# A new order of work for ScalarE, VectorE and TensorE in the SSD mixers of a four-layer encoder kernel

## The chip, the cores and the metric

The kernel runs on one core of one Trainium2 chip. The metric is the device time of one execution in microseconds (us); less is better. The instruction streams of the engines are written out by hand, one per engine, and meet only at semaphores, so each engine works strictly through its own list.

## The reference

A trunk of four layers over 256 tokens of 1024 features, all in float32. Layer 0 and layer 3 use the bidirectional Mamba-2 SSD mixer, layer 1 a gated short convolution, layer 2 neighbourhood attention; each mixer and each squared-ReLU MLP (1024 to 4096 to 1024) is followed by a LayerNorm of the residual sum. Only the SSD mixer is touched:

```
zxbcdt = x @ w_in                       # 1024 -> 2048 (z) + 4096 (x, B, C) + 64 (dt)
xbc = silu(depthwise_conv(xbc, conv_w) + conv_b)       # 5 taps
dt  = softplus(dt_raw + dt_bias)                       # two directions, 32 heads
y   = ssd(xs, dt, a, B, C) forward + the same backward + d_skip * xs
y   = y * silu(z)                                      # the gate
out = grouped_rmsnorm(y, norm_w) @ w_out               # 8 groups of 256 channels
```

The SSD runs in two chunks of 128 tokens: inside a chunk through a decayed product of C and B, across chunks through a state.

## The kernel before

**Weight units.** All weights, 226 blocks of mostly 128 x 2048 floats (1 MB), pass through one pipeline in the order of `plan_units`. SyncE loads unit u into a ring of three `raw` buffers as soon as unit u - 3 has been split. ScalarE copies it to `w_high` (L997), VectorE writes the remainder `w_low` = raw - w_high (L1338); both rings have four slots, so the split of unit u waits until TensorE has finished unit u - 4 (`w_used`). Three matmuls (high x high, low x high, high x low) stand for one product of full precision. `split_to(u)` on either engine means: split all units up to u, here, in this place of the engine's list. A split is one instruction of some 2 us on each engine, and everything behind it in the list waits for it and for what it waits for.

**Accumulators.** A projection (`project`) of 48 matmuls fills one of two accumulator banks, `acc`; it is freed when its reader has taken it. `result(u)` gives that reader the bank: it first runs `split_to(u + 3)` and only then waits for unit u to be finished on TensorE.

**The SSD mixer** has eight groups. A group has the units z, bc (B and C), x and so (its two row blocks of the output weight). Unit order: dt, z0, bc0, x0, z1, bc1, x1, then z(i), bc(i), x(i), so(i-2) for i = 2 to 6, then bc7, x7, z7, so5, so6, so7. With group i's projections, TensorE's loop of step i (L845 to L857) does the inner work of group i-1:

- project z(i); `state_products` (L800, "cb"); `turn_xs` (L789, "xs", the transpose of the convolved x); project bc(i); `cross_chunk` (L811, "off"); `scan` (L824, "yg"); project x(i); `out_unit` of so(i-2) (L681, "y" banks); `turn_gated` of group i-1 (L835, "op").
- These five inner steps cb, xs, off, yg, op take turns in two banks `inner`. The bank of xs is the one that op of the group before has used, and it is freed when VectorE has read it in `gated_low` (`op_low`, L1488).
- In the last step (i = 7) there is no z projection in the loop; z7 comes after it, and op6, cb7, so5 (in two halves by token tile, t0 and t1), xs7, off7, yg7 follow, then so6 with op7 inside it, then so7 (`tail`).

**ScalarE in step i** (L1188 to L1208): z_tanh(i); copies of cb and xs of group i-1; `shift_decays(i)` (L1091); `start_conv` bc(i) (bank to `conv_pad`, L1062, and the first tap, L1068); tanh of bc; `squares(i-1)`, half of `decays(i)` (L1101), `normalise(i-1)` (L1138); `start_conv` x(i); the other half of decays; tanh of x; `split_to(x(i)+4)`; `gated_high(i-1)` (L1148). z_tanh and start_conv call `result`, so each has a split in front of it.

**VectorE in step i** (L1608 to L1621): silu_z(i) (with a split in front); `decayed_products(i-1)` (L1508 to L1522); `join_decays(i)` (L1498); `add_cross(i-1)` (L1532, L1537); a split, then the taps of bc(i) (L1468, eight instructions); `gate_scan(i-1)` (L1548, L1550); silu of bc(i) (L1480); a split, then the taps of x(i); silu of x(i); `split_to(x(i)+4)`; `gated_low(i-1)` (L1488). The splits before the taps are at L1460.

GpSimd scales xs for the state and for the token itself (L432), raises the mean squares to the power -1/2 and issues the loads of the decays E, whose source is a small table in DRAM that ScalarE stores early in the mixer (L1183).

```
def result(u):                       # ScalarE and VectorE alike
    split_to(u + 3)
    act.wait_ge(w_used, u + 1)
    return acc_of[u]
```

## Time and profile before

| | before |
|---|---|
| median of 3 runs | 1647.73 us (1646.65 to 1647.95) |
| the profiled execution: its own time | 1646.52 us |
| its span, first to last instruction | 1644.6 us |
| mean granted TensorE clock | 0.946 of 2.4 GHz |
| TensorE matmul busy | 1491.3 us (91%) |
| VectorE busy | 991.2 us (60%) |
| ScalarE busy | 767.6 us (47%) |
| first SSD mixer, up to its last output matmul | 0 to 327.5 us of the span |
| second SSD mixer, likewise | about 1141 to 1443.7 us |

Rows of a timeline give start (us), duration (us), engine, line, what is written from what, the number of merged instructions and, in brackets, the idle time of the engine before it and what ended it. "L1338" is line 1338 of the kernel. In rows of stretches the numbers after the length are the busy time and count of instructions of TensorE, its weight loads, VectorE, ScalarE and GpSimd, then the granted clock as a share of 2.4 GHz, the share of the DMA engines and GB/s. Below, xs1 means the transposes of `turn_xs` for group 1, and so on.

### The profile page before, as it was taken

What the parts mean: (1) busy time and instruction counts of PE and PEld (TensorE: products, weight loads), DVE (VectorE), ACT (ScalarE), POOL (GpSimd) and SP (SyncE); (2) the same over time, 40 slices, a digit from 0 to 9 for tenths busy, and PEclk for the clock granted to TensorE, in tenths of its full rate; (3) what the DMA queues carried; (4) which work ended last, traced back from release to release, by engine and by line L of the source; (5) the groups of instructions that cost most, each with busy time, mean ns of one, the idle gap of its engine ahead of it and who ended that gap; (6) DMA issues with size and microseconds to landing.
All of it is one profiled execution on the core that took longest, in us unless ns stands there. A gap on an engine that the chain in (4) does not pass through costs nothing.

```text
span 1644.6 us, 24792 instructions
## 1 busy us (share of the span) xinstructions
PE 1491.3 (91%) x9837; PEld 1379.9 (84%) x9837; DVE 991.2 (60%) x1227; ACT 767.6 (47%) x1103; POOL 163.9 (10%) x245
## 2 busy tenths in 40 slices
PE   6888887799999999999999999999878787799996
PEld 6877887599998999999899799998878787689995
DVE  4767766655456666555754465556776776665554
ACT  3666655344433434443355444433656664435441
POOL 1111110052231000000000000000111120000000
PEclk9899898899999999999999999999999988899998
DMA  7635543346674564555553345555644462336551
GB/s 220 183 126 154 172 138 127 102 147 200 207 218 156 188 210 143 187 195 205 170 171 121 102 138 183 194 203 151 190 152 132 152 179 103 122 110 205 205 179 52
DMA packets 198193, 266.98 MB, mean 162 GB/s; under 512 B 11768, under 2 KB 167824, under 8 KB 198080
## 3 DMA queue, kind: packets, MB, share of 16 engines
q1 hardware_dynamic: 188032, 237.53, 43.6%
q0 software_dynamic: 9200, 27.55, 6.3%
q8 instruction: 79, 1.29, 0.3%
q10 hardware_dynamic: 848, 0.32, 0.1%
q14 instruction: 34, 0.28, 0.1%
HBM read 264.19 MB, written 1.18 MB: 161 GB/s over the span
## 4 chain that ended last, share of the span: by engine, by line
PE 66%; DVE 18%; issue 8%; ACT 7%; DMA 1%; SPq 0%; DVEq 0%; POOL 0%; ACTq 0%
PE acc L557 31%; PE y L681 24%; DVE conv L1468 6%; DVE w_low L1338 6%; PE acc L570 4%; ACT w_high L997 3%; PE y L570 1%; PE inner L789 1%; DMA raw<-in_ssd_w_in 1%; PE inner L811 1%; DVE opT L1488 1%; DVE gate L1550 1%; DVE gate L1548 1%; DVE E L1532 1%; ACT square L1130 1%
## 5 line engine op out<-in xcount | busy, mean ns | idle before, releaser
L557 PE MATMUL acc<-xT,w_high 128*128 128x256 f32 (+1 forms) x3392 | 646.2, 292 | 2.7 <-DVE xT L1399 1.1
L1338 DVE TENSOR_TENSOR w_low<-raw,w_high 128x2048 fp32r<-128x2048 f32 (+1 forms) x226 | 513.1, 2275 | 175.3 <-ACT w_high L997 93.3
L557 PEld LDWEIGHTS acc<-xT,w_high 128*128 128x128 f32 x3392 | 557.3, 201 | 7.8 <-issue 3.5
L997 ACT ACTIVATE w_high<-raw 128x2048 fp32r<-128x2048 f32 (+1 forms) x226 | 428.1, 1898 | 204.5 <-PE y L681 75.4
L557 PE MATMUL acc<-xT,w_low 128*128 128x256 f32 (+1 forms) x1696 | 492.8, 291 | 0.0
L681 PE MATMUL y<-w_high,opT 128*128 128x512 f32 x1408 | 404.3, 397 | 7.9 <-DVE opT L1488 6.0
L557 PEld LDWEIGHTS acc<-xT,w_low 128*128 128x128 f32 x1696 | 339.9, 200 | 0.0
L681 PEld LDWEIGHTS y<-w_high,opT 128*128 128x128 f32 x1408 | 263.9, 191 | 61.4 <-issue 9.5
L681 PE MATMUL y<-w_low,opT 128*128 128x512 f32 x704 | 226.3, 396 | 0.0
L570 PE MATMUL acc<-w_high,xT 128*128 128x256 f32 (+1 forms) x960 | 188.5, 298 | 15.6 <-DVE xT L1399 9.3
L1354 DVE TENSOR_TENSOR opT<-conv,opT 128x512 fp32r<-128x512 f32 x56 | 39.0, 696 | 267.2 <-issue 236.6
L570 PEld LDWEIGHTS acc<-w_high,xT 128*128 128x128 f32 x960 | 160.3, 205 | 19.4 <-issue 16.0
L681 PEld LDWEIGHTS y<-w_low,opT 128*128 128x128 f32 x704 | 134.5, 191 | 29.0
L570 PE MATMUL acc<-w_low,xT 128*128 128x256 f32 (+1 forms) x480 | 141.5, 295 | 0.0
L1468 DVE SCALAR_TENSOR_TENSOR conv<-conv_pad,ssd_par,conv 128x256 f32<-128x256 f32 x256 | 104.1, 479 | 3.4 <-ACT conv L1068 3.4
L1037 ACT ACTIVATE conv<-acc 128x512 f32<-128x512 f32 x60 | 35.8, 597 | 149.3 <-PE acc L557 135.1
L409 POOL TENSOR_TENSOR small<-small,minus_half 128x1 f32<-128x1 f32 x16 | 15.9, 993 | 842.6 <-DVE small L1375 842.6
L570 PEld LDWEIGHTS acc<-w_low,xT 128*128 128x128 f32 x480 | 98.7, 206 | 0.0
L789 PE MATMUL inner<-ident,xsT 128*128 128x128 f32 x64 | 16.1, 400 | 81.0 <-DVE opT L1488 78.5
L789 PEld LDWEIGHTS inner<-ident,xsT 128*128 128x128 f32 x64 | 10.6, 202 | 87.1 <-issue 68.0
L1076 ACT ACTIVATE tanh<-conv 128x512 f32<-128x512 f32 x32 | 20.2, 631 | 135.4 <-DVE conv L1468 135.4
L1024 ACT ACTIVATE xT<-inner 128x512 fp32r<-128x512 f32 x32 | 18.1, 595 | 117.5 <-PE inner L647 117.1
(182 smaller groups left out, 1175.6 us busy)
## 6 DMA issues: line engine op xcount, KB each, us to landing
raw<-in_ffn_w_in SPq DMA_DIRECT2D x128, 512.0 KB, 4.6
raw<-in_ffn_w_out SPq DMA_DIRECT2D x128, 512.0 KB, 4.4
raw<-in_ssd_w_in SPq DMA_DIRECT2D x96, 512.0 KB, 5.1
E<-cumsum_dram POOLq DMA_DIRECT2D x32, 512.0 KB, 5.5
raw<-in_ssd_w_out SPq DMA_DIRECT2D x32, 512.0 KB, 5.8
raw<-in_sc_w_in SPq DMA_DIRECT2D x24, 512.0 KB, 4.6
raw<-in_na_w_qkv SPq DMA_DIRECT2D x24, 512.0 KB, 4.6
raw<-in_sc_w_out SPq DMA_DIRECT2D x8, 512.0 KB, 4.4
```

The source lines that it names most:

```text
L557: mm = nc.tensor.matmul(bank[:, c * SEQ:(c + 1) * SEQ][:, span], w[:, col:col + P], xT[:, k, low, span], start=(k == 0 and part == 0), sto ...
L570: mm = nc.tensor.matmul(bank[:, t * width:(t + 1) * width], xT[:, k, low, t * P:(t + 1) * P], w[:, k * width:(k + 1) * width], start=(k == ...
L681: mm = nc.tensor.matmul(Y[t][c][:, :], opT[:, o % ACTS, low, k, t * P:(t + 1) * P], w[:, k * D + c * 512:k * D + (c + 1) * 512], start=(fi ...
L789: mm = nc.tensor.transpose(bank[:, t * GW + c * P:t * GW + (c + 1) * P], xsT[:, m % 2, c, t * P:(t + 1) * P], ident[:, :])
L811: mm = nc.tensor.matmul(bank[:, t * GW:(t + 1) * GW], cross[m % 2][:, (1 - t) * P:(2 - t) * P], xs_end[:, (1 - t) * GW:(2 - t) * GW], star ...
L997: nc.scalar.activation(w_high[:, u % SPLIT, 0:k * c], raw[:, u % RAW, 0:k * c], ACT.Copy).then_inc(w_high_done, 1)
L1024: nc.scalar.activation(xT[:, 4 * half:4 * half + 4, 0, t * P:(t + 1) * P], bank[:, :].rearrange("p (k c) -> p k c", k=4), ACT.Copy).then_i ...
L1037: nc.scalar.activation(conv[:, o % 2, :, :], views(bank[:, :]), ACT.Relu).then_inc(relu_done, 1)
L1076: nc.scalar.activation(th[:, m % 2, :], src, ACT.Tanh, scale=scale).then_inc(tanh_done, 1)
L1338: V.tensor_tensor(w_low[:, u % SPLIT, 0:k * c], raw[:, u % RAW, 0:k * c], f(w_high[:, u % SPLIT, 0:k * c]), ALU.subtract).then_inc(w_low_d ...
L1354: V.tensor_tensor(low, src, high, ALU.subtract).then_inc(op_low, 1)
L1468: ins = V.scalar_tensor_tensor(out=y, in0=pad[:, c % 2, i, q:q + SEQ], scalar=tap(j, q, ct), in1=y, op0=ALU.mult, op1=ALU.add)
```

## The change

`result` is parted in `split_to` and a new `finished(u)`, which only waits for unit u. In the SSD mixers the readers of the accumulators (`start_conv`, `z_tanh`, `silu_z`) use `finished`, and `taps` has no split any more; the splits become calls of their own behind the reader, each of unit u + 4 behind the reading of unit u. `gated_high` and `gated_low` stand ahead of the splits of step i. At both ends of the mixer the order changes: group 0 is transposed (op0) in step 2, behind z2; the last step is written out, with bc7 ahead of cb6 and x7 between xs6 and off6, and op6 behind the first half of so5. The other mixers and the MLP keep `result`.

```diff
 # TensorE
-                    for i in range(1, G):
-                        if i < G - 1:
-                            project(names[("z", i)], range(NT))
+                    for i in range(1, G - 1):
+                        project(names[("z", i)], range(NT))
+                        if i == 2:
+                            turn_gated(0)
                         state_products(i - 1)
                         turn_xs(i - 1)
                         project(names[("bc", i)], range(NT))
                         cross_chunk(i - 1)
                         scan(i - 1)
                         project(names[("x", i)], range(NT))
-                        if i < G - 1:
-                            if i >= 2:
-                                out_unit(s, names[("so", i - 2)], first=(i == 2))
+                        if i >= 2:
+                            out_unit(s, names[("so", i - 2)], first=(i == 2))
                             turn_gated(i - 1)
+                    project(names[("bc", G - 1)], range(NT))
+                    state_products(G - 2)
+                    turn_xs(G - 2)
+                    project(names[("x", G - 1)], range(NT))
+                    cross_chunk(G - 2)
+                    scan(G - 2)
                     project(names[("z", G - 1)], range(NT))
-                    turn_gated(G - 2)
                     state_products(G - 1)
+                    turn_xs(G - 1)
                     o = n["opu"]
                     n["opu"] += 1
                     out_part(s, names[("so", G - 3)], o, False, False, [0])
-                    turn_xs(G - 1)
-                    out_part(s, names[("so", G - 3)], o, False, False, [1]).then_inc(w_used, 1)
+                    turn_gated(G - 2)
                     cross_chunk(G - 1)
                     scan(G - 1)
+                    out_part(s, names[("so", G - 3)], o, False, False, [1]).then_inc(w_used, 1)
                     out_unit(s, names[("so", G - 2)], between=lambda: turn_gated(G - 1))
 # ScalarE (start_conv and z_tanh: finished in place of result)
+                    split_to(names[("dt", 0)] + 4)
                     z_tanh(0)
-                    split_to(names[("bc", 0)] + 3)
...
                     start_conv("bc", 0)
...
+                    split_to(names[("z", 0)] + 4)
                     conv_tanh()
+                    split_to(names[("bc", 0)] + 4)
                     start_conv("x", 0)
+                    split_to(names[("x", 0)] + 4)
                     conv_tanh()
                     shift_decays(0)
                     for i in range(1, G):
                         if i < G - 1:
                             z_tanh(i)
-                        if i == 1:
-                            decays(0, early)
-                            decays(0, late)
+                            if i == 1:
+                                decays(0, early)
+                                decays(0, late)
+                            if i == 2:
+                                gated_high(0)
+                        else:
+                            start_conv("bc", i)
+                            split_to(names[("bc", i)] + 4)
                         copy_cross(i - 1)
                         copy_xs(i - 1)
+                        if i < G - 1:
+                            split_to(names[("z", i)] + 4)
                         shift_decays(i)
-                        start_conv("bc", i)
-                        conv_tanh()
+                        if i < G - 1:
+                            start_conv("bc", i)
+                            split_to(names[("bc", i)] + 4)
+                            conv_tanh()
+                        else:
+                            conv_tanh()
+                            start_conv("x", i)
                         squares(i - 1)
                         decays(i, early)
                         normalise(i - 1)
-                        start_conv("x", i)
+                        if i < G - 1:
+                            start_conv("x", i)
                         decays(i, late)
+                        split_to(names[("x", i)] + 4)
                         conv_tanh()
-                        split_to(names[("x", i)] + 4)
                         if i == G - 1:
-                            z_tanh(G - 1)
-                        gated_high(i - 1)
-                    copy_cross(G - 1)
-                    copy_xs(G - 1)
-                    split_to(names[("so", G - 1)] + 1)
+                            z_tanh(i)
+                            copy_cross(i)
+                            copy_xs(i)
+                            split_to(names[("z", i)] + 4)
+                        if i >= 2:
+                            gated_high(i - 1)
+                            split_to(names[("so", i - 2)] + 4)
                     squares(G - 1)
                     normalise(G - 1)
-                    split_to(names[("so", G - 1)] + 2)
                     gated_high(G - 1)
 # VectorE (silu_z: finished in place of result; taps: no split)
...
+                    split_to(names[("dt", 0)] + 4)
                     silu_z(0)
-                    split_to(names[("bc", 0)] + 3)
                     dve.wait_ge(cs_acc, mixer + 1)
...
+                    split_to(names[("z", 0)] + 4)
                     silu_bc(0, taps("bc", 0))
-                    silu_x(0, taps("x", 0))
+                    split_to(names[("bc", 0)] + 4)
+                    y = taps("x", 0)
+                    split_to(names[("x", 0)] + 4)
+                    silu_x(0, y)
...
                     for i in range(1, G):
                         if i < G - 1:
                             silu_z(i)
...
+                            if i == 2:
+                                gated_low(0)
+                            decayed_products(i - 1)
+                            split_to(names[("z", i)] + 4)
+                            join_decays(i)
+                            add_cross(i - 1)
+                            y = taps("bc", i)
+                            gate_scan(i - 1)
+                            silu_bc(i, y)
+                            split_to(names[("bc", i)] + 4)
+                        else:
+                            y = taps("bc", i)
+                            decayed_products(i - 1)
+                            split_to(names[("bc", i)] + 4)
+                            silu_bc(i, y)
+                            join_decays(i)
+                            add_cross(i - 1)
+                            gate_scan(i - 1)
                         silu_x(i, taps("x", i))
-                        split_to(names[("x", i)] + 4)
                         if i == G - 1:
-                            silu_z(G - 1)
-                        gated_low(i - 1)
-                    decayed_products(G - 1)
-                    split_to(names[("so", G - 1)] + 1)
+                            silu_z(i)
+                            split_to(names[("x", i)] + 4)
+                            decayed_products(i)
+                            split_to(names[("z", i)] + 4)
+                        if i >= 2:
+                            gated_low(i - 1)
+                            if i < G - 1:
+                                split_to(names[("x", i)] + 4)
+                            split_to(names[("so", i - 2)] + 4)
+                        else:
+                            split_to(names[("x", i)] + 4)
                     add_cross(G - 1)
                     gate_scan(G - 1)
-                    split_to(names[("so", G - 1)] + 2)
                     gated_low(G - 1)
```

## Rows read from the trace of the kernel before

**Rows 1.** Stretches of the second mixer (xs1 to xs2, ...) and of an MLP
```profile
core 0: us, PE busy (x) PEld busy (x) DVE busy (x) ACT busy (x) POOL busy (x), PEclk, DMA share, GB/s
...
1214.89:1247.91 33.02, 28.81 (x200) 27.26 (x201) 21.91 (x37) 20.28 (x39) 4.17 (x6) 0.92 0.40 128
...
1349.58:1383.63 34.05, 24.12 (x153) 22.57 (x153) 23.93 (x38) 17.97 (x37) 5.26 (x6) 0.80 0.45 155
1383.63:1418.28 34.65, 27.20 (x188) 26.16 (x189) 21.82 (x37) 18.43 (x38) 2.93 (x4) 0.84 0.28 93
1418.28:1443.67 25.39, 22.01 (x88) 17.40 (x88) 14.09 (x23) 6.74 (x11) 3.73 (x5) 0.83 0.37 123
400.00:500.00 100.00, 100.00 (x623) 90.58 (x622) 54.17 (x39) 44.37 (x36) 29.70 (x47) 1.00 0.70 208
```

**Rows 2.** TensorE's timeline in a group of the first mixer: the inner steps
```profile
208.09 1.03 PE L811 MATMUL inner<-ring_a,E 128*128 128x256 f32 x4
...
221.97 0.60 PE L835 MATMUL inner<-ident,gate 128*128 128x128 f32 x4
...
228.15 1.03 PE L800 MATMUL inner<-ring_a 128*128 128x256 f32 x4
233.37 1.09 PE L789 MATMUL inner<-ident,xsT 128*128 128x128 f32 x4 [4.19 <-DVE opT L1488]
```

**Rows 3.** VectorE's timeline in the same group
```profile
201.91 1.22 DVE L1508 TENSOR_TENSOR E<-E,inner 128x1024 f32<-128x1024 f32 x1
...
203.98 1.33 DVE L1498 COPY_PREDICATED E<-suffix,E 128x1024 f32<-128x1024 uint32 x1
...
212.69 3.25 DVE L1468 SCALAR_TENSOR_TENSOR conv<-conv_pad,ssd_par,conv 128x256 f32<-128x256 f32 x8
...
222.13 2.29 DVE L1338 TENSOR_TENSOR w_low<-raw,w_high 128x2048 fp32r<-128x2048 f32 x1 [4.26 <-issue]
224.34 3.25 DVE L1468 SCALAR_TENSOR_TENSOR conv<-conv_pad,ssd_par,conv 128x256 f32<-128x256 f32 x8
228.37 0.69 DVE L1480 SCALAR_TENSOR_TENSOR xsT<-tanh,conv 128x512 f32<-128x512 f32 x1 [0.78 <-ACT tanh L1076]
230.15 2.29 DVE L1338 TENSOR_TENSOR w_low<-raw,w_high 128x2048 fp32r<-128x2048 f32 x1 [1.08 <-ACT w_high L997]
232.36 0.87 DVE L1488 SCALAR_TENSOR_TENSOR opT<-inner,ssd_par,opT 128x256 fp32r<-128x256 f32 x2
```

**Rows 4.** ScalarE's timeline in the same group
```profile
220.14 1.90 ACT L997 ACTIVATE w_high<-raw 128x2048 fp32r<-128x2048 f32 x1
221.95 0.57 ACT L1062 ACTIVATE conv_pad<-acc 128x512 f32<-128x512 f32 x1
222.56 1.10 ACT L1068 ACTIVATE conv<-conv_pad,ssd_par 128x256 f32<-128x256 f32 x2
...
228.17 1.89 ACT L997 ACTIVATE w_high<-raw 128x2048 fp32r<-128x2048 f32 x1
229.97 0.82 ACT L1148 ACTIVATE opT<-inner,ssd_par 128x256 fp32r<-128x256 f32 x2
```

**Rows 5.** Stretches: x(i) with yg's end; bc(i) behind the wait; so(i-2); z(i+1)
```profile
210.66:216.37 5.71, 5.71 (x49) 1.00 0.65 189
200.08:207.97 7.89, 7.89 (x50) 0.69 0.89 261
216.49:221.97 5.48, 5.48 (x27) 1.00 0.45 182
222.32:228.15 5.83, 5.83 (x51) 1.00 0.40 111
```

**Rows 6.** DMA issues: size each, median us from issue to landing
```profile
raw<-in_ssd_w_in SPq DMA_DIRECT2D x96, 512.0 KB, 5.1
```

**Rows 7.** VectorE's timeline in the second mixer: a split at its start, one at its end
```profile
1161.83 2.29 DVE L1338 TENSOR_TENSOR w_low<-raw,w_high 128x2048 fp32r<-128x2048 f32 x1 [0.82 <-issue]
...
1421.89 2.38 DVE L1338 TENSOR_TENSOR w_low<-raw,w_high 128x2048 fp32r<-128x2048 f32 x1 [1.69 <-issue]
```

More of the change, by code:

```diff
@@ L998, in split_to, with finished @@
                                          ACT.Copy).then_inc(w_high_done, 1)
+            def finished(u):
+                act.wait_ge(w_used, u + 1)
+                return acc_of[u]
             def result(u):
                 split_to(u + 3)
-                act.wait_ge(w_used, u + 1)
-                return acc_of[u]
+                return finished(u)
             def operand(o):
@@ L1058, in start_conv @@
                         n["conv"] += 1
-                        bank = result(names[(kind, g)])
+                        bank = finished(names[(kind, g)])
                         if c >= 2:
@@ L1161, in z_tanh @@
                     def z_tanh(g):
-                        bank = result(names[("z", g)])
+                        bank = finished(names[("z", g)])
                         tanh_of(bank[:, :], 0.5)
@@ L1339, in split_to, with finished @@
                                     f(w_high[:, u % SPLIT, 0:k * c]), ALU.subtract).then_inc(w_low_done, 1)
+            def finished(u):
+                dve.wait_ge(w_used, u + 1)
+                return acc_of[u]
             def result(u):
                 split_to(u + 3)
-                dve.wait_ge(w_used, u + 1)
-                return acc_of[u]
+                return finished(u)
             def operand(o):
@@ L1459, in taps @@
                         n["conv"] += 1
-                        split_to(names[(kind, g)] + 3)
                         dve.wait_ge(first_tap, 2 * (c + 1))
@@ L1569, in silu_z @@
                         m = n0 + g
-                        bank = result(names[("z", g)])
+                        bank = finished(names[("z", g)])
                         if m >= 3:
```

6 lines of the change are left out of this document (removed).

## The prediction

> **What bounds the kernel now.** I read the stretches first. In an MLP TensorE is busy without a gap at the full clock, so nothing on the other engines matters there. In the SSD mixers it is busy for about 29 of 34 us per group and its granted clock is 0.90; VectorE has 23.9 us of work in a group, ScalarE 20.3 [rows 1]. So no engine is full there, and the stretch is set by a chain through several of them.
>
> The timelines show the chain. TensorE stops once per group, 4.19 us ahead of xs, until VectorE's `gated_low` (opT, L1488) has emptied the `inner` bank that xs needs [rows 2]. The bank was written by op, which started at 221.97; ScalarE reads it at 229.97 and VectorE at 232.36. Between stand works that have nothing to do with it: one w_high and one w_low ahead of the gated pair (228.17, 230.15), and one w_high ahead of the emptying of x's accumulator (220.14 to 221.95), for which VectorE's own split idles 4.26 us with the taps of x queued behind [rows 3, 4]. The stop costs twice: the bc projection behind it runs at a granted clock of 0.69 and takes 7.89 us where x takes 5.71 at 1.00 [rows 5].
>
> I count five intervals per mixer from xs1 to xs6 (33.02, then 101.67 for three, then 34.05), 34.65 from xs6 to xs7, and 25.39 from xs7 to the last output matmul [rows 1]. The first mixer has the same waits at the same places, so I work out the second and double.
>
> **The steady part.** No instruction is added or removed; four splits per group stay four. What TensorE itself needs for a group at the full clock, start to start: bc 5.76 (x's rate), off and yg 2.57 (208.09 to 210.66), x 5.83, so 5.48, op 0.35, z 5.83, cb 0.87 (off's like), xs 0.35 (op's like): 27.05 us [rows 2, 5].
>
> Then the chain in the new order, from the start T of one xs (step i). Each piece carries its queue's predecessors.
> - TensorE: bc ends at T+6.1, yg at 8.7, x at 14.5, so at 20.0, op at 20.35, z at 26.2, cb at 27.05.
> - ScalarE: copy_xs to 1.35, w_high of unit z+4 to 3.2, decay shifts (2.4) to 5.5, bc's bank emptied and first taps to 8.0, w_high to 9.9.
> - VectorE: after its w_low of z+4 (to 6.3) and `join_decays` (1.33, to 7.65) it meets off, does `add_cross` (two of 0.69) and starts bc's taps at 9.05; taps, gate and silu end at 14.2, and a w_low fills the wait for ScalarE (to 16.4). ScalarE squares, normalises and reaches x's bank at 16.5, since the w_high of 220.14 no longer stands ahead; first taps done 18.2 (0.57 and 1.10), taps 21.5, tanh and silu 22.95 (0.78 and 0.69), gated pair 23.85 [rows 3, 4].
> - xs may start at 23.85 and TensorE arrives at 27.05. So the 4.19 us wait is gone with 3.2 us to spare, and with it the slow clock: no gap is left in which it fell.
>
> Next late is VectorE itself. Its chain with ScalarE, from bc's taps of one group to those of the next: 14.8 to the end of the gated pair, two w_low 4.5, silu of z 0.65, the decayed products 2.1 (201.91 to 203.98), a w_low 2.2, join 1.35, cross 1.4: 27.0 us. That is a tie with TensorE's 27.05; it drifts into the 3.2 us of slack if a little slower. I take 27.05, because the slack covers four groups of a drift of 0.8.
>
> The moved splits put waits in new places. The w_low of x+4 and so+4 now end at T+28.3, 1.25 behind the next xs; behind them are queued silu of z (x needs its bank at T'+8.7) and the decayed products (yg needs them at T'+7.0, they are done at 4.0). Both cost nothing while bc runs beside them. Weights: each unit is split at least 9 us ahead of its use. SyncE's loads hang on w_low: the tightest is issued at 26.1 and its split due 9 us later, against 5.1 us to landing [rows 6]. GpSimd's two products have to end by T+6.1 and the decays are loaded a group ahead; its queue gets nothing new. A group moves 5 MB with its decays, 185 GB/s in 27 us, where the MLP moves 208 [rows 1].
>
> Gains: the interval xs1 to xs2 stays slow at its front (below), 27.05 + 2.05 = 29.1 instead of 33.02, so 3.9; three at 101.67 - 81.15 = 20.5; xs5 to xs6 34.05 - 27.05 = 7.0. Together 31.4 us.
>
> **The start.** The w_low of bc1 (1161.83, 2.29 long, waiting 0.82) goes from ahead of the cumulative sums' copy to ahead of bc0's taps [rows 7]. TensorE's transposes of the sums come 3 us earlier, but bc0's taps do not: VectorE now waits for a w_high that ScalarE does behind bc0's first taps, and then splits itself. The taps start 1.0 later, and a second w_low (z2) stands ahead of the silu of x0, 1.4 net. I get xs0 2.4 us later, an idle TensorE of 8 us before it and a cold bc1. Then it is paid back: the split ahead of bc1's taps is gone (taps at the old time), the w_high ahead of x1's bank is gone (-2.4), and in step 2 the gated pair has one w_low and a silu ahead, without their 1.1 us wait: xs1 3.1 us earlier than 1214.89, after 5 us of idle.
>
> **The end.** From xs5 = 0. xs6 at 27.0. VectorE then has bc7's taps 28.3 to 31.5, decayed products, w_low of so6, silu, join, cross, gate (to 40.6), x7's taps to 43.8. ScalarE waits for that gate, then squares, decays, normalises, splits so7 and only then does x7's tanh at 47.3: silu 48.0, xs7 at 48.1, 21.1 behind xs6 instead of 34.65 (bc7 and the wait are ahead of xs6 now). Then half of so5 cold (to 53.4), op6; yg7 needs op6's bank, read by VectorE at 56.2 behind two w_low; the other half of so5 to 60.8. Here the change adds a wait: the split of unit so5+4 (fi1 of the MLP) wants so5 finished, w_high 62.8, w_low 65.1, and `add_cross(7)`, the gate and op7 are queued behind it; before, that place had a split that idled 1.69 us [rows 7]. op7 at 70.7, gated pair 73.2, so7 cold to 80.4. xs7 to the end takes 32.3 instead of 25.39: 6.9 lost; xs6 to the end is 53.4 instead of 60.04: 6.6 gained.
>
> **Sum.** 3.1 + 31.4 + 6.6 = 41.1 per mixer, 82.2 for both. The profiled execution took 1646.52 us with a span of 1644.6; the new span is 1562.4, the execution 1564.3. The median of the runs is 1.2 above the profiled one: 1565.5, of which I say 1565.
>
> **A rule against it.** The stop is regular and ends with the emptying of a PSUM bank. The Trainium skill, Perfetto Trace Analysis, section "Identifying Performance Opportunities", says that the same gap repeating on the engine that should be saturated can mean that there isn't enough SBUF or PSUM for the next tile; by that, order would not help, only a third bank, and the steady gain would be nothing. The trace speaks against it: of the 11.3 us between op's start and the bank's release, only 1.7 are the two reads [rows 2 to 4].
>
> **Rivals.**
> 1. *Only the turn is faster.* The splits behind the gated pair, or the tie on VectorE, give part of it back: the pair comes 3.4 us earlier (the two splits' 1.9 and 1.5), a short stop stays and the clock stays low behind it. 3.4 for each of five intervals, 17.0, with 9.7 at the ends: 26.7 per mixer, 1594. For it: VectorE's 27.0. Against: 3.2 us of slack at xs.
> 2. *The ends are better than I walked.* The walk leaves about 27 us of idle TensorE per mixer (8, 5, 6 ahead of xs7, 8 around op7). If a third of it goes, 18 us for both: 1547.
> 3. *Slower: the two banks are the bound.* If the release of op's bank still sets the period (34 us), what remains is xs0's 2.4 us not paid back and the 6.9 us that the wait on so5 adds ahead of `add_cross(7)`: 9.3 per mixer, 1666. It decides below a steady gain of 1.9 us per interval. It is what the rule above would give. Against it are the 11.3 us above.
> 4. *No change*, within 0.2% (3.3 us, about what a measurement can tell here): steady gain just 1.9 us. Nothing speaks for it.
>
> **Chances.** My forecast 0.74, rival 1 0.16, rival 2 0.05, rival 3 0.03, rival 4 0.02. Faster by over 0.2%: 0.95; same 0.02; slower 0.03. Range: my own case has ten walked intervals good to 1 us and the ends to 2 us each, so 1551 to 1580; rival 1 is taken in at the top, rival 2 in part. 1552 to 1596.
>
> **What would show it.** Right: xs to xs at 27 us with a granted clock of 1.00 from xs2 to xs6, no wait of TensorE on opT there; xs0 later by 2.4; xs7 waiting 5 to 6 us on the silu of x7, op7 waiting on the normalised gate for about 6 us, `add_cross(7)` right behind a w_low. Rival 1 shows a stop ahead of xs with a clock of 0.9; the tie shows as VectorE's idle time near zero. Rival 3 shows `gated_low` as late behind op as now. I am wrong if a load ends the idle time of w_high in the mixers, or if TensorE stops at another inner step than xs.

## The result and the profile after

The changed kernel takes 1598.47 us (median of 4 runs, 1588.08 to 1600.12) where the kernel before takes 1647.76 (4 runs, 1646.65 to 1647.95): a ratio of 0.9689, 95% interval 0.9648 to 0.973. It is faster, as forecast, but it is 33 us behind the 1565 forecast, and 2.5 us outside the range. A second series of the same kernel gave 1597.92 (1596.32 to 1599.24, 4 runs). The profiled execution of the first series is its fastest run, 1588.08, and this turns out to matter.

The head of its page, then the stretches of the second mixer that answer to [rows 1]: xs0 to xs1, xs1 to xs2, xs2 to xs3, xs3 to xs4, xs5 to xs6, xs6 to xs7, and xs7 to the last output matmul.

```profile
span 1586.2 us, 24792 instructions
...
PE 1470.3 (93%) x9837; PEld 1357.3 (86%) x9837; DVE 998.0 (63%) x1227; ACT 769.1 (48%) x1103; POOL 212.4 (13%) x245
```

```profile
core 0: us, PE busy (x) PEld busy (x) DVE busy (x) ACT busy (x) POOL busy (x), PEclk, DMA share, GB/s
1151.57:1183.06 31.49, 24.15 (x176) 23.62 (x177) 24.49 (x39) 21.62 (x49) 5.73 (x6) 0.88 0.42 136
1183.06:1212.16 29.10, 29.10 (x201) 27.84 (x201) 21.05 (x36) 20.18 (x38) 5.74 (x6) 0.92 0.42 144
1212.16:1239.28 27.12, 27.12 (x202) 25.85 (x200) 22.78 (x38) 19.35 (x38) 8.56 (x6) 1.00 0.61 194
1239.28:1268.09 28.81, 27.74 (x201) 25.73 (x200) 24.47 (x38) 20.06 (x40) 9.74 (x6) 1.00 0.57 183
...
1297.04:1326.01 28.97, 27.75 (x201) 25.75 (x201) 24.63 (x38) 20.34 (x40) 9.75 (x6) 1.00 0.53 182
1326.01:1351.37 25.36, 18.95 (x124) 18.21 (x124) 21.63 (x34) 16.64 (x37) 5.39 (x4) 0.86 0.38 125
1351.37:1386.24 34.87, 27.04 (x104) 21.60 (x104) 17.52 (x27) 7.81 (x13) 6.48 (x5) 0.76 0.28 91
```

What to see. TensorE is busy all through the second and the third stretch, the granted clock is 1.00 from xs2 to xs6, and a group takes 27.12 us where 27.05 was forecast. But only one interval is like that: the next ones take 28.8 to 29.0 (in the first mixer 28.8 to 29.2). And GpSimd, which has nothing new to do, is busy for 9.7 us of a group; in the kernel before it was 5.3 or less [rows 1], and over the span it went from 163.9 us to 212.4.

The difference of the spans is 58.4 us. I split it by the first transpose of the residual's tokens behind each mixer (L647): the first mixer ends 29.5 us earlier (299.19 against 328.68), the second takes 26.8 us less, and what lies between and behind them 2.1 less. Per mixer (first and second), gains against the sum of the prediction:

| part | forecast | measured |
|---|---|---|
| xs0, later by | 2.4 | 1.5, 2.3 |
| xs1, earlier by | 3.1 | 2.1, 1.2 |
| xs1 to xs6 | 31.4 | 25.5, 25.8 |
| xs6 to the end | 6.6 | 1.9, -0.2 |
| sum | 41.1 | 29.5, 26.8 |

The first row is not part of the sum, since the second already holds it. The second mixer is counted from the transposes of its tokens, the first from the start of the span. In eight profiles of kernels with the same start the first xs0 lies between 64.5 and 67.8 us, so the first figure of the first two rows is good to some 3 us only.

TensorE's waits in a steady group of the first mixer, and the two of the end. They answer to [rows 2].

```profile
188.34 1.10 PE L811 MATMUL inner<-ring_a,E 128*128 128x256 f32 x4 [0.29 <-DVE E L1539]
...
203.37 0.66 PE L835 MATMUL inner<-ident,gate 128*128 128x128 f32 x4 [0.92 <-ACT gate L1147]
...
210.67 0.63 PE L789 MATMUL inner<-ident,xsT 128*128 128x128 f32 x4
...
265.21 0.66 PE L789 MATMUL inner<-ident,xsT 128*128 128x128 f32 x4 [1.58 <-DVE xsT L1507]
...
288.15 1.12 PE L835 MATMUL inner<-ident,gate 128*128 128x128 f32 x4 [6.13 <-ACT gate L1147]
```

The 4.19 us stop ahead of xs is gone. In its place stand two short ones that the forecast did not have: 0.92 ahead of op, because the normalised gate is late, and 0.29 ahead of off. That TensorE would stop at another inner step than xs was one of the prediction's own signs of being wrong. The other one shows too: a load ends the idle time of w_high once in the steady part of each mixer, 0.81 us at 190.62 and 0.36 at 1305.53. Behind the first of them ScalarE then idles 4.89 us for VectorE's taps, so it is not what holds the group up. The 6.13 us ahead of op7 were forecast as about 6.

**Where the gate is lost.** GpSimd's timeline, then ScalarE's and VectorE's in the same group (step 5: xs4 at 181.67, xs5 at 210.67). L459 and L460 raise the mean squares of 128 x 2 numbers to a power. They answer to [rows 3, 4].

```profile
199.76 1.82 POOL L459 TENSOR_SCALAR small<-small 128x2 f32<-128x2 f32 x1 [6.97 <-ACT square L1139]
201.66 0.71 POOL L460 TENSOR_TENSOR small<-small,minus_half 128x2 f32<-128x2 f32 x1
```

```profile
202.41 0.91 ACT L1147 ACTIVATE gate<-gate,small 128x256 f32<-128x256 f32 x2 [1.57 <-POOL small L460]
203.22 0.58 ACT L1071 ACTIVATE conv_pad<-acc 128x512 f32<-128x512 f32 x1
```

```profile
198.64 0.68 DVE L1507 SCALAR_TENSOR_TENSOR ring_a<-tanh,conv 128x512 f32<-128x512 f32 x1
199.24 2.28 DVE L1363 TENSOR_TENSOR w_low<-raw,w_high 128x2048 fp32r<-128x2048 f32 x1
204.96 3.26 DVE L1495 SCALAR_TENSOR_TENSOR conv<-conv_pad,ssd_par,conv 128x256 f32<-128x256 f32 x8 [3.44 <-ACT conv L1077]
```

L459 does 256 elements in 1.82 us and ends as VectorE's w_low does. It is so in 12 of the 16 groups (1.81 or 1.82 us, each ending within 0.06 us of the w_low's end); in the other four, where no w_low runs beside it, it takes 0.19 or 0.21. In the kernel before, no w_low ran at that place:

```profile
218.30 0.19 POOL L459 TENSOR_SCALAR small<-small 128x2 f32<-128x2 f32 x1 [6.00 <-ACT square L1130]
```

So the w_low that the change puts behind the silu of bc holds up GpSimd, GpSimd the normalisation on ScalarE, this the emptying of x's bank, and that the taps of x on VectorE itself, which idles 3.44 us. That was the theory with which I went to the chip. Its rival was the prediction's own: VectorE's 27.0 us are a tie, and small losses add up.

### The profile page after: what moved, and what is told of

Its sections match the earlier page's. It is cut to its first block, busy times and chain, and to the rows that moved or that the text cites. A ratio compares the mean times of both kernels' runs of the same rounds, so it can differ in the third digit from the quotient of the medians.

```text
span 1586.2 us, 24792 instructions
## 1 busy us (share of the span) xinstructions
PE 1470.3 (93%) x9837; PEld 1357.3 (86%) x9837; DVE 998.0 (63%) x1227; ACT 769.1 (48%) x1103; POOL 212.4 (13%) x245
## 4 chain that ended last, share of the span: by engine, by line
PE 62%; DVE 22%; ACT 7%; issue 6%; POOL 2%; DMA 1%; SPq 0%; DVEq 0%; ACTq 0%; POOLq 0%
PE acc L557 28%; PE y L681 25%; DVE w_low L1363 6%; DVE conv L1495 6%; PE acc L570 4%; ACT w_high L1003 2%; POOL small L459 1%; DVE E L1525 1%; ACT square L1139 1%; PE y L570 1%; DVE E L1535 1%; DMA raw<-in_ssd_w_in 1%; POOL small L460 1%; DVE gate L1577 1%; DVE E L1564 1%
## 5 line engine op out<-in xcount | busy, mean ns | idle before, releaser
L557 PE MATMUL acc<-xT,w_high 128*128 128x256 f32 (+1 forms) x3392 | 624.3, 286 | 1.7 <-DVE xT L1427 1.1
L557 PEld LDWEIGHTS acc<-xT,w_high 128*128 128x128 f32 x3392 | 538.5, 195 | 6.6 <-issue 2.3
L557 PE MATMUL acc<-xT,w_low 128*128 128x256 f32 (+1 forms) x1696 | 483.6, 285 | 0.0
L557 PEld LDWEIGHTS acc<-xT,w_low 128*128 128x128 f32 x1696 | 329.5, 194 | 0.0
L570 PE MATMUL acc<-w_high,xT 128*128 128x256 f32 (+1 forms) x960 | 189.8, 299 | 14.2 <-DVE xT L1427 8.9
L681 PEld LDWEIGHTS y<-w_low,opT 128*128 128x128 f32 x704 | 134.5, 191 | 29.1
L1495 DVE SCALAR_TENSOR_TENSOR conv<-conv_pad,ssd_par,conv 128x256 f32<-128x256 f32 x256 | 105.7, 485 | 41.2 <-ACT conv L1077 41.2
L432 POOL TENSOR_TENSOR ring_a<-ring_b,decay_to_end 128x512 f32<-128x512 f32 x16 | 33.2, 2076 | 187.6 <-ACT ring_b L1130 168.8
L496 POOL DMA_DIRECT2D E<-in_na_rpb x64 | 34.1, 538 | 92.3 <-ACT conv L1046 91.2
```

What stands on the lines that cost most here:

```text
L432: return nc.gpsimd.tensor_tensor(spread(dst, shape), spread(tri_b[:, n % 2, :], shape), factors, ALU.mult)
L496: pool.dma_start(dst, src).then_inc(window_landed[h % WINDOW_BUFS], 16)
L557: mm = nc.tensor.matmul(bank[:, c * SEQ:(c + 1) * SEQ][:, span], w[:, col:col + P], xT[:, k, low, span], start=(k == 0 and part == 0), sto ...
L570: mm = nc.tensor.matmul(bank[:, t * width:(t + 1) * width], xT[:, k, low, t * P:(t + 1) * P], w[:, k * width:(k + 1) * width], start=(k == ...
L681: mm = nc.tensor.matmul(Y[t][c][:, :], opT[:, o % ACTS, low, k, t * P:(t + 1) * P], w[:, k * D + c * 512:k * D + (c + 1) * 512], start=(fi ...
L1495: ins = V.scalar_tensor_tensor(out=y, in0=pad[:, c % 2, i, q:q + SEQ], scalar=tap(j, q, ct), in1=y, op0=ALU.mult, op1=ALU.add)
```

## The experiments

Each is compared with runs of the kernel before on the same chip. Intervals are given as first mixer | second mixer.

**The same kernel again.**

> The changed kernel once more, for the spread of its time (1588.08 to 1600.12 in four runs, where the kernel before keeps within 1.3 us) and for a second profile. If the 10 us come from the clock, the profile of a slower run shows one of the stops with more of the work behind it at the low level and the same waits; if they come from a wait (the tie on VectorE falling one way or the other), the intervals from xs3 to xs6 differ from the 28.8 to 29.2 us of the first profile.

Measured: 1597.92 (1596.32 to 1599.24, 4 runs), ratio 0.9702 [0.9689, 0.9715], span 1594.4. All intervals inside the mixers are those of the first profile within 0.3 us, but for the 34.87 at the second mixer's end, which is 32.5 here, so that the end gains 2.1 in both mixers. What is longer, by 9.7 us, lies between the mixers, in layer 1, the short convolution. TensorE's granted clock there, in this profile (TensorE's columns alone) and in the first one (all engines, as in [rows 1]):

```profile
core 0: us, PE busy (x), PEclk, DMA share, GB/s
498.00:501.00 3.00, 1.93 (x18) 1.00 0.39 156
501.00:504.00 3.00, 3.00 (x20) 0.65 0.00 0
504.00:507.00 3.00, 3.00 (x16) 0.50 0.93 294
...
519.00:522.00 3.00, 3.00 (x16) 0.50 0.00 0
522.00:525.00 3.00, 3.00 (x26) 0.93 0.30 85
```

```profile
501.00:504.00 3.00, 3.00 (x30) 3.00 (x28) 3.00 (x2) 0.71 (x1) 0.00 (x0) 1.00 0.10 21
504.00:507.00 3.00, 3.00 (x29) 3.00 (x29) 0.93 (x2) 2.40 (x2) 0.00 (x0) 1.00 1.07 367
```

Both have the same gap ahead of this, 1.07 us behind the LayerNorm, at 499.23 in the one and at 498.49 in the other. In the second profile the clock falls to 1.2 GHz behind it and stays there for some 20 us while TensorE is busy without a pause. The same matmuls then take 9.6 us more. Nothing that the change touches runs there. By its size this also accounts for the difference between 1588.08 and the three other runs of the first series, and so for 10 us of the median: their mean granted clock is 0.960, as in this series (0.959 to 0.960), against 0.966 in the run of 1588.08. They were not profiled.

**Take the w_low out of GpSimd's way.** VectorE waits for L460 ahead of the split behind the silu of bc; nothing else is changed.

```diff
                             silu_bc(i, y)
+                            dve.wait_ge(rms_done, n0 + i)
                             split_to(names[("bc", i)] + 4)
```

> VectorE waits for GpSimd's power (rms_done) ahead of the w_low behind the silu of bc. Theory A, the shared port: L459 takes 1.82 us because that w_low runs beside it, and the normalise, the bank of x and its taps are late by 1.6 us; then L459 is back at 0.2 us, the wait of TensorE ahead of op (0.9 us) is gone, the intervals from xs3 to xs6 fall from 29.0 to 27.1 to 27.6, and the time by 8 to 14 us. Rival B, VectorE simply has too much in its chain: the w_low is 1.4 us later, the intervals stay at 29 or grow by up to 1.4 us, time the same to 14 us more.

Measured: 1568.11 (1566.08 to 1576.92, 5 runs), ratio 0.953 [0.9506, 0.9554]. xs1 to xs2 28.91 | 29.81, then 27.12 in all eight intervals to xs6, xs6 to xs7 21.7 | 21.7. VectorE in the group that answers to the one above, and the totals of L459 (16 groups: busy us, mean ns, idle before) in the kernel before, the changed kernel and this one:

```profile
196.54 2.29 DVE L1363 TENSOR_TENSOR w_low<-raw,w_high 128x2048 fp32r<-128x2048 f32 x1 [1.46 <-POOL small L460]
199.10 3.26 DVE L1495 SCALAR_TENSOR_TENSOR conv<-conv_pad,ssd_par,conv 128x256 f32<-128x256 f32 x8 [0.26 <-ACT conv L1077]
```

```profile
L459 POOL TENSOR_SCALAR small<-small 128x2 f32<-128x2 f32 x16 | 3.1, 192 | 117.3 <-ACT square L1130 117.3
```

```profile
L459 POOL TENSOR_SCALAR small<-small 128x2 f32<-128x2 f32 x16 | 22.6, 1413 | 110.8 <-ACT square L1139 110.8
```

```profile
L459 POOL TENSOR_SCALAR small<-small 128x2 f32<-128x2 f32 x16 | 3.1, 194 | 92.1 <-ACT square L1139 92.1
```

An added wait makes the kernel 20 us faster than the profiled run of the changed kernel, 17.4 from profile to profile and 30 by the medians; 8 to 14 were expected. VectorE idles 1.46 us for it and saves 3.2 us ahead of the taps; of all waits ahead of taps on the first taps of ScalarE, 41.2 us in the changed kernel, 3.2 are left. L459 is back at 0.19 to 0.21 us in all 16 groups, and TensorE has no stop left between xs2 and xs6. The theory stands. The rival falls: with VectorE's own work unchanged, even 1.5 us longer by the wait, the group takes 27.12 us four times in a row.

The stretching goes the other way too, and this remains. VectorE's `join_decays` took 1.33 us in the kernel before [rows 3]. In the changed kernel it starts while GpSimd's second product of xs is under way:

```profile
188.67 3.02 POOL L432 TENSOR_TENSOR ring_b<-ring_b,own_token 128x512 f32<-128x512 f32 x1 [1.84 <-DVE own_token L1549]
```

```profile
190.71 2.23 DVE L1525 COPY_PREDICATED E<-suffix,E 128x1024 f32<-128x1024 uint32 x1
```

It takes 2.18 to 2.23 us in the seven groups of the changed kernel where it meets the product, 2.15 to 2.17 in the eight groups with the added wait, and 1.28 to 1.36 where it does not meet it. The prediction had it at 1.33 to 1.35. With the wait there is room for these 0.8 us; nobody waits for the product itself.

**Put the split of unit so5+4 behind the last gate.** On ScalarE behind `normalise(7)`, on VectorE behind `gate_scan(7)`, where the kernel before has a split too.

```diff
 # VectorE (ScalarE likewise, behind normalise(G - 1))
                             if i < G - 1:
                                 split_to(names[("x", i)] + 4)
-                            split_to(names[("so", i - 2)] + 4)
+                                split_to(names[("so", i - 2)] + 4)
...
                     gate_scan(G - 1)
+                    split_to(names[("so", G - 3)] + 4)
```

> The last split of the mixer (unit so5+4) stands behind the last gate on VectorE and behind the last normalise on ScalarE. Theory: the 7.0 us idle time of VectorE ahead of that w_low and the w_low itself hold add_cross(7), the gate, and so op7, for which TensorE waits 6.1 us; then VectorE starts add_cross(7) as soon as GpSimd's own_xs is there, TensorE's wait ahead of op7 falls to below 1 us, and so7 starts at the full clock: 6 to 8 us per mixer, 12 to 16 in all. Rival: the stop only moves to so7, whose gated pair now has the split in front of it: 2 to 4 us per mixer.

Measured: 1573.74 (1571.99 to 1575.58, 4 runs), ratio 0.9556 [0.9543, 0.9569]. VectorE at the end of the first mixer, in the changed kernel and in this one:

```profile
280.05 2.29 DVE L1363 TENSOR_TENSOR w_low<-raw,w_high 128x2048 fp32r<-128x2048 f32 x1 [7.04 <-ACT w_high L1003]
282.26 0.68 DVE L1559 TENSOR_TENSOR E<-inner,decay_from_end 128x512 f32<-128x512 f32 x1
```

```profile
275.58 0.68 DVE L1561 TENSOR_TENSOR E<-inner,decay_from_end 128x512 f32<-128x512 f32 x1
...
284.17 2.29 DVE L1365 TENSOR_TENSOR w_low<-raw,w_high 128x2048 fp32r<-128x2048 f32 x1 [4.84 <-ACT w_high L1003]
```

VectorE idled 7.04 us for ScalarE's w_high, which waited 6.77 us for so5 on TensorE; `add_cross(7)`, the gate and op7 stood behind. With the split moved, op7 has no wait, and 0.9 us are left ahead of so7. From xs6 to the end it takes 51.8 | 51.8 us against 59.2 | 59.1 in the second profile of the changed kernel: 7.4 | 7.3 us. The steady intervals are unchanged. The rival, that the stop only moves to so7, has 0.9 us of it right. The median fell by 24 us: some 15 from the two ends, the rest because none of these runs has the fall of the clock (by their mean granted clocks, 0.970 to 0.972).

**One part alone.** The kernel before with nothing but the gated pair ahead of the split of x(i)+4, in steps 1 to 6.

```diff
-                        split_to(names[("x", i)] + 4)
                         if i == G - 1:
+                            split_to(names[("x", i)] + 4)
                             silu_z(G - 1)
                         gated_low(i - 1)
+                        split_to(names[("x", i)] + 4)
```

> The kernel before with one part of the change alone: the gated pair ahead of the split of unit x(i)+4. My walk: the pair comes 3.4 us earlier, the stop ahead of xs falls from 4.2 to 0.8 us and the bc behind it stays at the full clock as long as the stop is that short: 34.0 becomes 28.5 to 30.6 us per interval, 1602 to 1615 us in all. If the splits in front of the accumulators are what matters, the stop only changes its place (to the silu of x) and the time stays above 1630.

Measured: 1598.82 (1598.28 to 1600.28, 4 runs), ratio 0.9709 [0.9696, 0.9722]. TensorE in a steady group:

```profile
184.08 0.63 PE L789 MATMUL inner<-ident,xsT 128*128 128x128 f32 x4 [1.44 <-DVE opT L1489]
...
191.83 1.10 PE L811 MATMUL inner<-ring_a,E 128*128 128x256 f32 x4 [1.37 <-DVE E L1513]
```

The steady intervals are 30.33 to 30.35 us, with a stop of 1.44 ahead of xs and one of 1.37 ahead of off. Turning two calls round gives the same median as the whole change, a little less than the 1602 to 1615 expected. This version has no fall of the clock in its profile and none of the new end's wait, and its clock in the steady groups is 1.00 as well; the fair comparison is 30.3 us per group against 27.1, 28.8 and 29.0. The larger part of the stop was the place of two splits; the splits behind the bank readers are worth 3.2 us more per group once GpSimd is out of the way, and half of that or less when it is not.

**Both repairs.** The edits of the wait on GpSimd and of the late last split together.

> The changed kernel with both edits: VectorE waits for GpSimd's power ahead of the w_low behind the silu of bc, and the last split stands behind the last gate. If the two causes are separate, their gains add: 27.12 us per interval from xs2 to xs6 and 21.7 from xs6 to xs7 as with the first edit, and about 6 us less from xs7 to the last output matmul in each mixer as with the second: 12 us less than the first edit alone, 1554 to 1560. If they share a cause, it stays within 4 us of the better one, 1564 to 1568.

Measured: 1552.43 (1550.76 to 1567.6, 6 runs), ratio 0.9436 [0.9409, 0.9462]. From the changed kernel without the fall of the clock (1588.08) the two edits take 20.0 and 14.3 us; together 35.7, a little more than was expected (1554 to 1560). They add. Five runs lie between 1550.8 and 1553.3, one at 1567.6, with a mean granted clock of 0.964 against 0.973 or more; it was not profiled, and it is 15 us slower, more than the 10 that the fall cost where it was seen.

**The start: taps of bc0 ahead of the second split.**

```diff
+                    y = taps("bc", 0)
                     split_to(names[("z", 0)] + 4)
-                    silu_bc(0, taps("bc", 0))
+                    silu_bc(0, y)
```

> The changed kernel with the taps of bc0 ahead of the split of bc1 on VectorE, for the 3.6 us idle time ahead of that w_low (it waits for a w_high that stands behind bc0's first taps on ScalarE). Theory, as in the prediction's start: the taps begin 4.1 us earlier, the silu of bc0 1.9 us earlier (the w_low now stands between), x0's taps and xs0 1.5 to 2 us earlier, and about the same at xs1: 2 to 4 us in all. Rival: the w_low only moves, and ScalarE's chain (w_high of x1, first taps of x0) sets xs0: within 1 us of the changed kernel.

Measured: 1580.65 (1578.44 to 1589.45, 6 runs), ratio 0.959 [0.9577, 0.9602]; five of the six are at 1578 to 1582, and the profiled one, 1589.45, has the fall of the clock behind the same 1.07 us gap. VectorE at the start of the second mixer in the changed kernel, and the same taps here:

```profile
1135.23 2.29 DVE L1363 TENSOR_TENSOR w_low<-raw,w_high 128x2048 fp32r<-128x2048 f32 x1 [3.61 <-issue]
1137.44 3.25 DVE L1495 SCALAR_TENSOR_TENSOR conv<-conv_pad,ssd_par,conv 128x256 f32<-128x256 f32 x8
```

```profile
1140.74 3.26 DVE L1495 SCALAR_TENSOR_TENSOR conv<-conv_pad,ssd_par,conv 128x256 f32<-128x256 f32 x8 [1.76 <-ACT conv L1077]
1143.92 2.29 DVE L1363 TENSOR_TENSOR w_low<-raw,w_high 128x2048 fp32r<-128x2048 f32 x1
```

In the changed kernel the taps stand behind a w_low for which VectorE idles 3.61 us; here they start as soon as ScalarE has the first taps (1.76 us of idle time), and the w_low runs while ScalarE does the tanh. The idle time of TensorE ahead of xs0 is 3.49 | 4.24 us instead of 7.40 | 8.13 in the second profile of the changed kernel, 3.9 less each, and the execution is about 8 us shorter, where 2 to 4 were expected. Nothing of it is given back at xs1.

**The old end.** The changed kernel with the last step (i = 7) in the order of the kernel before on all three engines, the last split behind the gate as there, steps 1 to 6 new.

```diff
 # TensorE
-                    project(names[("bc", G - 1)], range(NT))
                     state_products(G - 2)
                     turn_xs(G - 2)
-                    project(names[("x", G - 1)], range(NT))
+                    project(names[("bc", G - 1)], range(NT))
                     cross_chunk(G - 2)
                     scan(G - 2)
+                    project(names[("x", G - 1)], range(NT))
                     project(names[("z", G - 1)], range(NT))
+                    turn_gated(G - 2)
                     state_products(G - 1)
...
```

> The changed kernel with the last step (i = 7) in its old order on all three engines, with the last split behind the last normalise and gate as before; steps 1 to 6 stay. It prices the new end: from xs5 to the last output matmul the kernel before takes 94.1 us, the changed one 89.2 (second mixer). If the new order is worth its 6.6 us of my walk, this one takes 6 us more per mixer than the changed kernel, 1608 to 1612. If the wait on so5 takes back what the order brings, it is the same or faster, 1585 to 1600, with xs6 to the end at 56 to 60 us.

Measured: 1580.26 (1578.67 to 1582.22, 4 runs), ratio 0.9592 [0.9579, 0.9604]. From xs6 to the end it takes 54.0 | 53.9 us, against 59.2 | 59.1 in the changed kernel and 51.8 | 51.8 with the new order and the late split. (In the old order bc7 stands behind xs6 and in the new one ahead of it, but xs5 to xs6 takes the same 29.2 | 29.0 in all three, so the comparison holds.) So the new order of the last step alone is worth 2.1 us per mixer, and the early split in it costs 7.4: as it came, the new end is 5.2 us per mixer worse than the old one would have been behind the new steady part. The time is below both ranges that were expected for it (1585 to 1600, 1608 to 1612).

**All three repairs.** The wait on GpSimd, the late last split, the taps first at the start.

> All three edits in the changed kernel, as the fastest version that the experiments point to: the sum of theirs, 1551 to 1558; with the port theory wrong somewhere, no better than the two edits together.

Measured: **1546.07** (1544.22 to 1557.2, 5 runs), ratio 0.9394 [0.9372, 0.9416]; the fastest of all versions. From 1588.08 the three edits alone take 20.0, 14.3 and about 8 us (1580 without the fall): 42 together, as this run has it. It is below the 1551 to 1558 expected, which took the third edit at its forecast 2 to 4 us. Four runs are at 1544 to 1546.5, one at 1557.2.

**What makes the clock fall in layer 1.** The changed kernel with 12, then 24 more transposes (their results are not used) in the MLP of layer 0, which put the gap 1.3 and 2.6 us further behind the first mixer's end than in the first profile.

```diff
                         project(names[("fi", b)], range(NT))
+                        if s == 1 and b == 9:
+                            for _ in range(12):
+                                nc.tensor.transpose(I[0][:, 0:P], ident[:, :], ident[:, :])
```

> The changed kernel with 12 transposes of the identity into a bank that is free there, in the middle of layer 0's MLP (their result is not used): everything behind them, the short-convolution mixer with its fall of the clock at 502 us among it, comes about 1 us later and is otherwise the same. Theory: whether the clock falls behind the 1.1 us gap at the start of the short convolution is a matter of where the gap lies in time, since the same gap does not make it fall in the first profile and in the kernel before; then most runs lose the fall, 1587 to 1590, or keep it, 1597 to 1601, and this kernel and the one shifted by twice as much need not agree. Rival: the fall belongs to the changed kernel's work there (its waits or data); then both shifted kernels stay at 1598 to 1602.

Measured: 1590.22 (1588.07 to 1595.26, 4 runs), ratio 0.9663 [0.9645, 0.9681]. The stretch behind the gap, which ends at 501.56 here:

```profile
501.00:504.00 3.00, 2.44 (x22) 1.00 0.20 57
504.00:507.00 3.00, 3.00 (x29) 1.00 0.11 18
```

> The same with 24 transposes, about 2 us later. Theory: as above, 1588 to 1591 where the fall is gone; rival: 1599 to 1602.

Measured: 1592.49 (1590.0 to 1593.74, 5 runs), ratio 0.9667 [0.9654, 0.968]. The clock is 1.00 from 495 to 525 here too.

With more work in it the kernel is faster: seven of the nine shifted runs are below 1593 and the highest is 1595.26, where seven of the eight unshifted ones lie at 1596.3 to 1600.1. So the gap's length does not decide (1.06 or 1.07 us in all profiles). Of the eleven profiles of changed kernels, the fall stands behind the gaps that end at 496.42 and 499.23, and not behind those that end at 478.53, 482.50, 491.29, 493.60, 495.48, 498.49, 501.56, 503.47 and 505.05. That the gap's moment decides fits this, but it is not shown: the shifted kernels ran on another chip than the second series of the changed kernel, and the unshifted one was never run on that chip, where the kernel before is 1.6 us faster too. Nor does one kernel behave alike in all its runs on one chip. What the moment would have to meet stays open. The shifted kernels are still 2 to 4 us above 1588.08: the transposes themselves are part of it, and the first mixer ends at 300.92 and 301.55 instead of 299.19, within the scatter of the start, which I did not pursue.

## Why the prediction was right and wrong

**Right.** The stop ahead of xs was a matter of order, not of banks: no bank was added, and the wait on opT is gone from the steady part (rival 3 falls, and with it the reading of this stop by the rule behind it). TensorE's own need, 27.05 us, was measured as 27.12. xs1 to xs2 is 29.1 in the second mixer, as forecast. xs6 to xs7 takes 21.7 us once GpSimd is out of the way; 21.1 was the walk. With the wait the gated pair ends at T+23.9 and leaves the 3.2 us of slack ahead of xs that were forecast. xs0 is 1.5 | 2.3 us later, forecast 2.4 (counted from the tokens' transposes ahead of the second mixer), with 7.5 | 8.1 us of idle TensorE ahead of it, forecast 8; ahead of xs1 it idles 8.1 | 7.3, forecast 5. `add_cross(7)` stands behind a w_low that waits 7.04 us, and op7 waits 6.13.

**Wrong, first: the chain of VectorE and ScalarE, "27.0 us, a tie", with 3.2 us of slack at xs.** Every link was priced from rows in which the neighbours ran as before. The link "ScalarE squares, normalises" goes through GpSimd, and the forecast gave GpSimd one sentence: "its queue gets nothing new". Its queue got nothing new, but its instruction got a neighbour. L459 went from 0.19 us to 1.82. The walk has the silu of bc done at T+14.2 and x's taps at T+21.5: with the wait on GpSimd they are done at T+14.3 and T+21.6 (xs at 180.75); in the changed kernel at T+17.6 and T+26.5 (xs at 181.67). Against the forecast, 5.9 | 5.6 us of the steady 31.4 are missing, and some of both ends: xs6 to xs7 is 25.4 instead of 21.1, xs1 comes 2.1 | 1.2 us early instead of 3.1. Measured with this one repair, the whole is 1568.1, 3 us from the forecast, and the steady gain 32.0 | 30.4. The chain had a second price wrong for the same reason, `join_decays` at 1.35 instead of 2.2 us, which cost nothing once the first was mended.

By the Trainium skill, GPSIMD Engine Reference, section "Specifications", GpSimd's interfaces to SBUF are shared with VectorE, and there is contention with VectorE instructions that have two SBUF inputs. w_low is one (raw and w_high). The runs agree: L459 takes 1.82 us with it beside the instruction and 0.19 without; the 1413 ns above are the mean over 12 groups of the one kind and four of the other. This rule bore on the change, and the prediction weighed another one.

**Wrong, second: the end, 6.6 us per mixer; it gave 2.1 at most.** The price of the wait on so5 was right (about 6 us ahead of op7, measured 6.13). What failed is the walk from xs6 to xs7, 21.1 us, measured 25.4. L459 itself takes 0.21 us there. But VectorE comes out of the last steady group late: in the first mixer bc7's taps start 4.2 us behind xs6, where the forecast had 1.3, and GpSimd's first product runs beside them, so that they take 4.04 us:

```profile
244.02 4.04 DVE L1495 SCALAR_TENSOR_TENSOR conv<-conv_pad,ssd_par,conv 128x256 f32<-128x256 f32 x8
```

With the wait on GpSimd they start 1.3 behind xs6 and take 3.25, xs6 to xs7 is 21.7, and the end gains 4.8 | 3.6. The rest of the end, xs7 to the last output matmul, takes 33.5 | 34.7 there, where the walk had 32.3; which link of it is short was not followed.

**Wrong, third: everything outside the mixers was taken as unchanged, at a cost of nothing.** The 41.1 us per mixer were taken off the time of an execution in which layer 1 ran at full clock, and only 1.2 us were put between it and the median. In seven of eight runs of the changed kernel the clock fell in layer 1, by the times, and this costs 10 us where it was seen. Nothing in the profile of before announces this: a gap of the same length is harmless there.

**The parts add up.** 33 us are missing in the median: 10 are the fall of the clock; 20 are GpSimd's stretched instruction, by the run that takes it away (17.4 from profile to profile); the remaining 3 are what that run still lacks. By its profile the mixers gain 37.3 | 36.9 of the 41.1, 8.0 us too little, 4.8 of them at the two ends and 2.6 at the start of the first mixer, where the start scatters; 1.7 are gained outside them, and its median lies 2.6 below its profiled run, where the forecast put the median 1.2 above. That the 10 us of the unprofiled runs are the same fall as in the profiled one is argued from their size and their mean granted clock. Rival 1 has the time nearly right, 1594, but not its mechanism: no stop ahead of xs remained, and the clock was not low. Its short stop is what the kernel with the one part alone shows, 1.44 us ahead of xs and 1598.8, though the clock stayed at 1.00 there too. That its number is near the changed kernel's is luck.

**What the forecast held for unavoidable.** The idle times it walked ahead of xs0 and op7 were right in size, and both were one misplaced split each. Rival 2, that a third of this idle time goes, gives 1547, and the repaired kernel takes 1546.07. But it was said of the kernel without repairs, so this is no confirmation.

## What to carry to other kernels

When work moves on VectorE, ask what GpSimd does in the same microseconds, even where it is only 256 elements long: look at the mean time of its small instructions before and after, and if another engine waits for one, try a wait ahead of VectorE's long instruction. Price VectorE's own instructions, too, from rows in which GpSimd does what it will do then. A split, a copy or anything else without a reader in a hurry belongs behind the instruction that someone waits for, and ahead of it only if it cannot wait itself; a call that waits for a unit's end (so5) never ahead of the gate on which the next unit hangs. And before a median is compared with a sum, look for a stretch that the change does not touch and that is longer all the same.

## What the runs showed of the hardware that was not expected

- A GpSimd instruction of 128 x 2 elements takes 192 to 194 ns alone and 1.81 to 1.82 us in the 12 groups in which a 128 x 2048 VectorE subtraction with two SBUF inputs runs beside it; it then ends with the subtraction. The subtraction itself kept its mean (2299 ns against 2289 before, 2295 with the wait).
- The scaling of xs on GpSimd (L432, 128 x 512) went from a mean of 1102 ns to 2076 for the first product and from 1548 to 2405 for the second, for the same reason as far as the timelines show; nobody waits for these. With the added wait the first is back at 1231, the second is at 2530.
- VectorE's 128 x 1024 COPY_PREDICATED takes 1.28 to 1.36 us alone and 2.15 to 2.23 in the 15 groups of the two profiles in which it starts while such a product is running. In all these cases it is the instruction that starts second that is stretched.
- Behind one and the same 1.07 us gap TensorE's granted clock can stay at 1.00 or fall to 0.50 for some 20 us of uninterrupted matmuls. What decides is open: 24 transposes of useless work ahead of it, 2.6 us, went with a median 6 us lower, but on another chip.
